# Two transformer blocks on one core: the feed-forward input takes its high weights over both halves of the activations in one product of 512 columns

## The chip, the cores and the metric

The kernel runs on one core of a Trainium2 chip. A time is the device time of one execution in microseconds (us), lower is better; three executions of the kernel before gave 1177.74, 1178.14 and 1179.59 us, so its median is 1178.14 us. The profile is of one further execution, with a time of its own.

## The reference, cut to what matters

Two transformer blocks follow each other on 256 tokens of width 1024. The first has a gated mixer, an attention and a lookup of expert rows; the second has three mixer branches and a feed-forward layer. Only that last layer is touched:

```python
n2 = rmsnorm(h, norm_ffn_pre[l])                                  # 256 x 1024
gu = n2 @ w_ffn_in[l]                                             # 1024 x 5632
ff = (jax.nn.silu(gu[..., :D_FF]) * gu[..., D_FF:]) @ w_ffn_out[l]  # D_FF = 2816
h = h + rmsnorm(ff, norm_ffn_post[l])
```

## The kernel before

**Split products.** Every weight and activation of the large products is float32 and is split in two: a high part, rounded to the type fp32r of TensorE (written by ScalarE, `w_hi`, `nT_hi`, `hT_hi`), and a low part, the rest (written by VectorE as a difference, `w_lo`, `nT_lo`, `hT_lo`). A product is three matmuls into one place of PSUM: high by high, high weights by low values, low weights by high values (`product`, L1818 to L1823).

**Weight blocks.** Weights come in blocks of 128 x 2048 numbers (1 MB). SP (the queue of SyncE) loads each into one of four slots of `wraw`, as soon as the block that stood there is split (`load_block`, L586). ScalarE rounds a block into one of three slots of `w_hi` (L772, "the cast") and VectorE writes `w_lo` beside it (L1228). The cast of a block must wait until TensorE has done with the block that used the slot three blocks earlier. TensorE starts a block when its `w_lo` is written (`w_split`).

**Feed-forward input.** There are 22 blocks `ff_in0` to `ff_in21`. Block j holds 128 channels of the gate half (a = 0) and 128 channels of the other half (a = 1, called "up" here), each with 8 chunks of 128 inputs. `channels_out` writes both into one PSUM bank, gate in columns 0 to 255 and up in columns 256 to 511; channels are on the partitions and the 256 tokens are the columns. Then ScalarE takes the silu of the gate (L1160), VectorE multiplies by the up half (`h32`, L1762, "the product" below), ScalarE rounds it (`hT_hi`, L1164, "the copy") and VectorE writes the rest (`hT_lo`, L1766).

**Order on ScalarE and VectorE.** Both execute strictly in the order in which the code issues. One turn j of the loop on ScalarE (L1155 to L1166) is: silu j, copy j - 1, cast of the block three places after `ff_in`j. One turn on VectorE (L1755 to L1769) is: product j, rest j - 1, `w_lo` of the block three places after. After turn 19 these blocks are `ff_out0`, `ff_out1` and so on.

**Feed-forward output.** 11 blocks `ff_out0` to `ff_out10`, each 24 matmuls of 512 columns (`rows_out`). Then the last norm and the store.

PSUM has eight banks; `psum_uses` hands them out in turn and `bank_full` / `bank_read` count for each bank how often it was filled and read. The kernel's functions around the change:

Of the kernel before, what the change touches and what calls it, by code (L numbers as in the profile page):

```python
# [13 lines left out]
P = 128  # L14
D = 1024
S = 256
# [62 lines left out]
def last_product(name):  # L79

    base, part = name[:-1], name[-1]
    if name in ("in2_x", "x_o"):
        return ("xq",) if name == "in2_x" else ("y_x", NT - 1, 1)
    if name.startswith(("in2_q", "in2_k")):
        return (name[4:5] + "2", int(part))
    if name.startswith("ff_in"):
        return ("ff", int(name[5:]))
    if name.startswith("ff_out"):
        return ("ff_out", NT - 1, 1) if name == f"ff_out{FC // 2 - 1}" else None
    if name.startswith(("pool_o", "sb_o")):  # L90
        return ("y_" + base[:-2], NT - 1, 1) if part == "1" else None
    if name in ("out1a", "out1b"):
        return ("w_out", 1, NT - 1) if part == "b" else None
    if part == "a":
        return None
    if name.startswith("in2_g"):
        return ("gate", int(name[5:-1]), NT - 1)
    if name in ("in2_vb", "in2_pb"):
        return (("v2", NT - 1) if name == "in2_vb" else ("pool_in", NT - 1))
    if name.startswith("out2_"):  # L100
        return ("w_out2", int(name[5:-1]), NT - 1)
    return ("proj" if name.startswith("in") else "w_out", int(name[-2]), NT - 1)
# [35 lines left out]
def psum_uses():  # L138

    uses, count, turn, held = {}, [0] * 8, {}, set()  # L140

    def use(*key, among=tuple(range(8))):
        free = [b for b in among if b not in held]
        n = turn.get(among, 0)
        while among[n % len(among)] not in free:
            n += 1
        b = among[n % len(among)]
        turn[among] = n + 1
        uses[key] = (b, count[b])
        count[b] += 1  # L150
        return b

    def both(name):
        for t in range(NT):
            for h in range(2):
                use(name, t, h)

    both("xT")
    for n in (1, 2, 3, 4):
        for t in range(NT):  # L160
            use("proj", n, t)
    for t in range(NT):
        for name in ("qT", "kT"):
            use(name, t)
    held.add(use("proj", 0, 0))
    use("score", 0)
    use("score", 1)
    held.add(use("proj", 0, 1))
    use("score", 2)
    use("pT", 0)  # L170
    use("pT", 1)
    held.remove(uses["proj", 0, 0][0])
    use("spatial", 0)
    for u in (3, 4):
        use("score", u)
    first = use("oT", 0)
    use("aT", 0)
    held.add(use("w_out", 0, 0))
    held.remove(uses["proj", 0, 1][0])
    use("pT", 2)  # L180
    use("score", 5)
    use("spatial", 1)
    held.add(use("w_out", 1, 0))
    for key in (("xbT", 0, 0), ("aT", 1), ("query0", 0), ("xbT", 0, 1), ("query0", 1)):
        use(*key)
    held.clear()
    use("pT", 3)
    use("route0")
    for key in (("w_out", 0, 1), ("w_out", 1, 1), ("oT", 1)):
        held.add(use(*key))  # L190
    for key in (("pT", 4), ("pT", 5), ("query1",), ("route1",)):
        use(*key)
    held.clear()
    for n in range(2):
        held.add(use("expert", 0, n))
    for h in range(2):
        use("xbT", 1, h)
    for j in [*range(EARLY, PEER_HEADS), *range(EARLY)]:
        use("query", j)
        use("route", j)  # L200
    first = set(held)
    for n in range(2):
        held.add(use("expert", 1, n))
    both("memT")
    use("mk")
    use("mv")
    held -= first
    both("nT")
    for t in range(NT):
        use("v2", t)  # L210
    held.clear()
    for key in ("q2", "k2"):
        for c in range(2):
            use(key, c)
    z_banks, sum_banks, one = (0, 1, 2, 3), (4, 5, 6), (7,)
    for i, name in enumerate(SLOT_BLOCKS):
        if pair_at(i, ATT_SLOT) is not None:
            use("sbT", pair_at(i, ATT_SLOT), among=one)
        if pair_at(i, Z_SLOT) is not None:
            for a in range(2):  # L220
                use("z", 2 * pair_at(i, Z_SLOT) + a, among=z_banks)
        if i in XS_SLOT:
            for j in range(2):
                use("xs", XS_SLOT.index(i), j, among=z_banks)
        if i in MIX_SLOT:
            use("mix", MIX_SLOT.index(i), among=one)
        if i in POOL_SLOT:
            use("poolT", POOL_SLOT.index(i), among=one)
        for h in heads_at(i, XO_SLOT)[::2]:
            use("xoT", h // 2, among=z_banks)  # L230
        for h in heads_at(i, XPT_SLOT):
            use("xpT", h, among=z_banks)
        if name == "in2_x":
            use("xq", among=sum_banks)
        elif name[-1] == "a":
            for t in range(NT):
                use(*slot_key(name, t), among=sum_banks)
    for key in ("y_x", "y_pool", "y_sb"):
        for t in range(NT):
            for n in range(2):  # L240
                use(key, t, n)
    both("mergedT")
    for t in range(NT):
        for n in range(2):
            use("w_out2", n, t)
    both("n2T")
    for j in range(FC):
        use("ff", j)
    for t in range(NT):
        for n in range(2):  # L250
            use("ff_out", t, n)
    return uses
# [26 lines left out]
def two_block_kernel(nc, io, out):  # L279
# [7 lines left out]
    with ExitStack() as ctx:  # L287
# [3 lines left out]
        def sem(name):  # L291
            return ctx.enter_context(nc.semaphore(name))
# [28 lines left out]
        def place(name, off, shape, dt=F32):  # L321
            size = 4
            for n in shape[1:]:
                size *= n
            assert off + size <= arena_bytes, name
            return nc.alloc_sbuf_tensor_at(name, shape, dt, offset=first_byte + off)
# [48 lines left out]
        w_apart = {"query2": (apart_prob[:, 1, :], apart_end[:, 2, :]), "query3": (apart_prob[:, 0, :], apart_prob[:, 2, :]),  # L375
                   "query6": (apart_keys[:, 0, :], apart_keys[:, 1, :]), "query7": (apart_end[:, 0, :], apart_end[:, 1, :])}

        nT_hi = place("nT_hi", 102 * KB, [P, KC, S], F32R)
        nT_lo = place("nT_lo", 110 * KB, [P, KC, S], F32R)
        gates = place("gates", 48 * KB, [P, NT, 3 * D])  # L380
        xqT = place("xqT", 70 * KB, [P, 2, S])
        sbT_hi = place("sbT_hi", 72 * KB, [P, 4, S], F32R)
# [20 lines left out]
        z_sb = place("z_sb", 92 * KB, [P, NT, D])  # L403
        silu = place("silu", 118 * KB, [P, 2, S])
        h32 = place("h32", 120 * KB, [P, 2, S])

        mkT = mkv[:, 0:2, :]
        mv = mkv[:, 2:4, :]
# [88 lines left out]
        h_ready = sem("h_ready")  # L497
        half_n2 = sem("half_n2")
        silu_ready = sem("silu_ready")
        product_rounded = sem("product_rounded")  # L500
        ffT_ready = sem("ffT_ready")

# [54 lines left out]
        def wait_full(eng, *key):  # L557

            b, u = at(*key)
            eng.wait_ge(bank_full[b], u + 1)  # L560
            return bank[b]
# [150 lines left out]
        def _(act):  # L712
# [441 lines left out]
            split_to("ff_in2")  # L1154
            for j in range(FC + 1):  # L1155
                if j < FC:
                    src = wait_full(act, "ff", j)
                    if j >= 2:
                        wait_read(act, "ff", j - 2)
                    nc.scalar.activation(silu[:, j % 2, :], src[:, 0:S], ACT.Silu).then_inc(silu_ready, 1)  # L1160
                if j >= 1:

                    wait_read(act, "ff", j - 1)
                    nc.scalar.copy(hT_hi[:, j - 1, :], h32[:, (j - 1) % 2, :]).then_inc(product_rounded, 1)  # L1164
                if j < FC:
                    split_ahead(f"ff_in{j}")  # L1166
# [12 lines left out]
        def _(dve):  # L1179
# [572 lines left out]
            for h in range(2):  # L1752
                rest_tile("n2T", nT_lo, nT_hi, 1, h)
            split_to("ff_in2")
            for j in range(FC + 1):  # L1755
                if j < FC:

                    dve.wait_ge(silu_ready, j + 1)
                    if j >= 2:
                        dve.wait_ge(ffT_ready, j - 1)  # L1760
                    src = bank[at("ff", j)[0]]
                    nc.vector.tensor_tensor(h32[:, j % 2, :], silu[:, j % 2, :], src[:, S:2 * S],  # L1762
                                            ALU.mult).then_inc(read_of("ff", j), 1)
                if j >= 1:
                    dve.wait_ge(product_rounded, j)
                    nc.vector.tensor_tensor(hT_lo[:, j - 1, :], h32[:, (j - 1) % 2, :], hT_hi[:, j - 1, :].bitcast(F32),  # L1766
                                            ALU.subtract).then_inc(ffT_ready, 1)
                if j < FC:
                    split_ahead(f"ff_in{j}")  # L1769
# [10 lines left out]
        def _(pe):  # L1780
# [503 lines left out]
                            turn_n2(0)  # L2284
            keep_warm(22, "n2T", 1, 0)
            turn_n2(1)
            for j in range(FC):
                channels_out(f"ff_in{j}", nT, "ff", j, turned="n2T" if j == 0 else None)
            for j in range(FC // 2):
                pe.wait_ge(ffT_ready, 2 * j + 2)  # L2290
                rows_out(f"ff_out{j}", (hT_hi, hT_lo), j == 0, j == FC // 2 - 1, 2 * j, lambda t, n: ("ff_out", t, n))
# [101 lines left out]
```

## Time and profile before

| quantity | value |
|---|---|
| median of three executions | 1178.14 us (1177.74 to 1179.59) |
| profiled execution, its own time | 1177.23 us |
| span of its trace | 1175.4 us |
| feed-forward input on TensorE, first matmul | 983.09 us from the start of the span |
| feed-forward output on TensorE, first and last matmul | 1109.89 and 1169.52 us |
| granted clock of TensorE, mean of the execution | 0.994 |

In what follows PE is TensorE, PEld its weight loads, DVE is VectorE, ACT is ScalarE, POOL is GpSimd. Times inside the execution count from the start of the span. Durations of matmuls in the profile are modelled and overlap each other; how fast TensorE works is read from the distance between starts. On DVE and ACT too, one instruction may start a little before the one ahead of it has ended in the records.

### The profile page before, as it was taken

The page shows a single profiled execution, that of the slowest core. Times are in us where ns is not written, and L with a number is a line of the kernel's source. Part 1 is how long each engine was busy: PE and PEld are TensorE (multiplying, and loading weights), DVE is VectorE, ACT ScalarE, POOL GpSimd, SP SyncE. Part 2 cuts the span into 40 slices and gives each one's busy share as a digit, 9 for nine tenths or more (in the row PEclk, how much of TensorE's full clock was granted, in tenths as well). Part 3 has the DMA queues.
Part 4 walks back from the last instruction along what each step waited for, and adds up shares of the span by engine and source line. Part 5 has one row for each costly group of instructions (what it writes and reads, how often), then busy time and mean ns, then how long its engine had stood idle before and what let it go on. Part 6 is the DMA issues. An engine that isn't in the chain of part 4 may idle for free.

```text
span 1175.4 us, 12637 instructions
## 1 busy us (share of the span) xinstructions
PE 1060.0 (90%) x4468; PEld 689.4 (59%) x4468; DVE 811.2 (69%) x1704; ACT 389.8 (33%) x724; POOL 272.4 (23%) x261
## 2 busy tenths in 40 slices
PE   8999699999998778798877777899999999999998
PEld 7888354544454233244322222359888878999986
DVE  5787868777877768787887776764555586555543
ACT  7674212202220111310211012045765445444532
POOL 0001345434444334433433433400000000000000
PEclk9999899999999999999999999999999999999999
DMA  9847999999999999999999999977434444555540
GB/s 346 337 168 270 393 375 398 422 421 421 422 420 422 421 421 421 421 421 421 418 420 422 410 421 416 421 271 267 144 143 144 162 161 161 180 180 181 183 174 36
DMA packets 55534, 371.91 MB, mean 316 GB/s; under 512 B 6192, under 2 KB 7344, under 8 KB 12080
## 3 DMA queue, kind: packets, MB, share of 16 engines
q0 software_dynamic: 36864, 268.45, 55.4%
q1 hardware_dynamic: 18608, 102.65, 23.7%
q8 instruction: 36, 0.59, 0.2%
q14 instruction: 26, 0.21, 0.0%
HBM read 370.03 MB, written 1.05 MB: 316 GB/s over the span
## 4 chain that ended last, share of the span: by engine, by line
PE 58%; DMA 29%; DVE 8%; issue 3%; ACT 1%; POOL 1%; DVEq 0%; POOLq 0%; ACTq 0%
DMA uv<-in_peer_uv,eidx 29%; PE bank L2123 13%; PE bank L1821 12%; PE bank L1823 12%; PE bank L1822 12%; PE bank L1893 4%; DVE uv L1509 3%; PE bank L1792 1%; DVE diag L1523 1%; POOL uv L696 1%; PE bank L2011 1%; DVE xn L1691 0%; DVE tmp L1684 0%; PE bank L1965 0%; PE bank L1932 0%
## 5 line engine op out<-in xcount | busy, mean ns | idle before, releaser
L2123 PE MATMUL bank<-uv,diag 128*128 128x512 f32 x1024 | 491.2, 608 | 100.4 <-DVE diag L1523 93.9
L1509 DVE SCALAR_TENSOR_TENSOR uv<-uv,xn 128x1024 f32<-128x1024 f32 x256 | 313.5, 1225 | 132.4 <-DMA uv<-in_peer_uv,eidx 129.9
L2123 PEld LDWEIGHTS bank<-uv,diag 128*128 128x128 f32 x1024 | 180.4, 191 | 375.9 <-issue 373.5
L696 POOL DMA_INDIRECT uv<-in_peer_uv,eidx x256 | 272.1, 1063 | 485.6 <-PE bank L2123 357.6
L1228 DVE TENSOR_TENSOR w_lo<-wraw,w_hi 128x2048 fp32r<-128x2048 f32 x71 | 162.3, 2290 | 119.5 <-ACT w_hi L772 119.4
L984 ACT ACTIVATE chosen<-chosen 128x1 f32<-128x1 f32 x256 | 51.8, 203 | 505.0 <-DVE uv L1509 504.7
L772 ACT CAST w_hi<-wraw 128x2048 fp32r<-128x2048 f32 x71 | 135.3, 1908 | 65.6 <-PE bank L1823 65.4
L1821 PE MATMUL bank<-nT_hi,w_hi 128*128 128x256 f32 x432 | 122.5, 284 | 0.8 <-DVE nT_lo L1249 0.8
L1822 PE MATMUL bank<-nT_lo,w_hi 128*128 128x256 f32 x432 | 122.3, 283 | 0.0
L1823 PE MATMUL bank<-nT_hi,w_lo 128*128 128x256 f32 x432 | 122.3, 283 | 0.0
L1523 DVE TENSOR_SCALAR diag<-const,chosen 128x128 f32<-128x128 f32 x256 | 89.1, 348 | 10.9 <-ACT chosen L984 10.7
L1821 PEld LDWEIGHTS bank<-nT_hi,w_hi 128*128 128x128 f32 x432 | 81.7, 189 | 1.2 <-issue 1.0
L1822 PEld LDWEIGHTS bank<-nT_lo,w_hi 128*128 128x128 f32 x432 | 81.7, 189 | 0.0
L1823 PEld LDWEIGHTS bank<-nT_hi,w_lo 128*128 128x128 f32 x432 | 81.7, 189 | 0.0
L1821 PE MATMUL bank<-w_hi,nT_hi 128*128 128x512 f32 x144 | 57.5, 399 | 0.3 <-DVE w_lo L1228 0.3
L1822 PE MATMUL bank<-w_lo,nT_hi 128*128 128x512 f32 x144 | 56.2, 390 | 0.0
L1823 PE MATMUL bank<-w_hi,nT_lo 128*128 128x512 f32 x144 | 56.1, 390 | 0.0
L1821 PE MATMUL bank<-w_hi,aT_hi 128*128 128x512 f32 x104 | 41.7, 401 | 2.3 <-DVE w_lo L1236 2.3
L1823 PE MATMUL bank<-w_hi,aT_lo 128*128 128x512 f32 x104 | 40.9, 393 | 0.0
L1822 PE MATMUL bank<-w_lo,aT_hi 128*128 128x512 f32 x104 | 40.8, 392 | 0.0
L1893 PEld LDWEIGHTS bank<-bT,wraw 128*128 128x128 f32 x192 | 30.3, 191 | 11.6 <-issue 9.7
L1893 PE MATMUL bank<-bT,wraw 128*128 128x128 f32 (+1 forms) x192 | 34.9, 327 | 0.0
(271 smaller groups left out, 1190.6 us busy)
## 6 DMA issues: line engine op xcount, KB each, us to landing
wraw<-in_ff_in SPq DMA_DIRECT2D x22, 1024.0 KB, 4.8
wraw<-in_ff_out SPq DMA_DIRECT2D x11, 1024.0 KB, 4.7
wraw<-in_query SPq DMA_DIRECT2D x4, 1024.0 KB, 5.2
uv<-in_peer_uv,eidx POOLq DMA_INDIRECT x256, 13.2
wraw<-in_in_q SPq DMA_DIRECT2D x2, 1024.0 KB, 9.0
wraw<-in_in_k SPq DMA_DIRECT2D x2, 1024.0 KB, 9.6
wraw<-in_pool_o SPq DMA_DIRECT2D x2, 1024.0 KB, 4.8
wraw<-in_sb_o SPq DMA_DIRECT2D x2, 1024.0 KB, 4.7
```

The lines of the kernel that those rows point to most:

```text
L696: pool.indirect_dma_start(out=uv[:, RING_AT[n % RING], :], out_offset=None, in_=io["peer_uv"], in_offset=bass.IndirectOffsetOnAxis(ap=eidx ...
L772: nc.scalar.copy(hi, raw).then_inc(w_rounded, 1)
L984: nc.scalar.activation(hgelu[head % 2][:, k:k + 1], hdot[head % 2][:, k:k + 1], ACT.Gelu_apprx_tanh).then_inc(hgelu_ready, 1)
L1228: nc.vector.tensor_tensor(lo, raw, hi.bitcast(F32), ALU.subtract).then_inc(w_split, 1)
L1509: nc.vector.scalar_tensor_tensor(out=u, in0=u, scalar=1.0, in1=xn[:, head // PEER_HEADS, :], op0=ALU.mult, op1=ALU.mult, accum_out=hdot[he ...
L1523: nc.vector.tensor_scalar(diag[:, n % RING, :], ident, hgelu[head % 2][:, k:k + 1], gate[head % 2][:, k:k + 1], ALU.mult, ALU.mult).then_i ...
L1792: mm = nc.tensor.transpose(dst[:, c * P:(c + 1) * P], src[:, c * P:(c + 1) * P], ident)
L1821: nc.tensor.matmul(dst, a_hi, b_hi, start=start, stop=False)
L1822: nc.tensor.matmul(dst, a_hi, b_lo, start=False, stop=False)
L1823: return nc.tensor.matmul(dst, a_lo, b_hi, start=False, stop=stop)
L1893: mm = nc.tensor.matmul(dst[:, a * width:(a + 1) * width], w[:, c * S + a * P:c * S + (a + 1) * P], aT[:, i % 2 * (KC // 2) + c, first:fir ...
L2123: mm = nc.tensor.matmul(acc[m][:, :], diag[:, n % RING, :], uv[:, RING_AT[n % RING], D + m * HALF:D + (m + 1) * HALF], start=(n % (ROWS // ...
```

## The change

High and low values now lie in one tile `nT_both` (same bytes as before; `nT_hi` and `nT_lo` are views of it). For a chunk, the high weights are used once, against high and low values together: one matmul of 2 x 256 = 512 columns. Its left 256 columns are high by high and its right 256 columns high weights by low values. The low weights make a second matmul of 256 columns that adds into the left half. The gate and the up half now take a bank each (44 uses of banks in place of 22). The two halves of a bank have to be summed: VectorE does that with one reduction per bank into `gate32` and `up32` in SBUF. The silu now reads `gate32`, the product reads `silu` and `up32`, and comes one turn later on VectorE than before.

```diff
@@ psum_uses
     for j in range(FC):
-        use("ff", j)
+        for a in range(2):
+            use("ff", j, a)
@@ ScalarE
             for j in range(FC + 1):
                 if j < FC:
-                    src = wait_full(act, "ff", j)
+                    wait_read(act, "ff", j, 0)
                     if j >= 2:
-                        wait_read(act, "ff", j - 2)
-                    nc.scalar.activation(silu[:, j % 2, :], src[:, 0:S], ACT.Silu).then_inc(silu_ready, 1)
+                        act.wait_ge(product_ready, j - 1)
+                    nc.scalar.activation(silu[:, j % 2, :], gate32[:, j % 2, :], ACT.Silu).then_inc(silu_ready, 1)
                 if j >= 1:
 
-                    wait_read(act, "ff", j - 1)
+                    act.wait_ge(product_ready, j)
                     nc.scalar.copy(hT_hi[:, j - 1, :], h32[:, (j - 1) % 2, :]).then_inc(product_rounded, 1)
@@ VectorE
-            for j in range(FC + 1):
+            for j in range(FC + 2):
                 if j < FC:
-
-                    dve.wait_ge(silu_ready, j + 1)
-                    if j >= 2:
-                        dve.wait_ge(ffT_ready, j - 1)
-                    src = bank[at("ff", j)[0]]
-                    nc.vector.tensor_tensor(h32[:, j % 2, :], silu[:, j % 2, :], src[:, S:2 * S],
-                                            ALU.mult).then_inc(read_of("ff", j), 1)
-                if j >= 1:
-                    dve.wait_ge(product_rounded, j)
-                    nc.vector.tensor_tensor(hT_lo[:, j - 1, :], h32[:, (j - 1) % 2, :], hT_hi[:, j - 1, :].bitcast(F32),
+                    for a, dst in ((0, gate32), (1, up32)):
+                        src = wait_full(dve, "ff", j, a)
+                        if not a and j >= 2:
+                            dve.wait_ge(silu_ready, j - 1)
+                            dve.wait_ge(product_ready, j - 1)
+                        nc.vector.tensor_reduce(dst[:, j % 2, :], src[:, :].rearrange("p (b k) -> p k b", b=2),
+                                                AX_X, ALU.add).then_inc(read_of("ff", j, a), 1)
+                if 1 <= j <= FC:
+                    dve.wait_ge(silu_ready, j)
+                    if j > 2:
+                        dve.wait_ge(ffT_ready, j - 2)
+                    wait_read(dve, "ff", j - 1, 1)
+                    nc.vector.tensor_tensor(h32[:, (j - 1) % 2, :], silu[:, (j - 1) % 2, :], up32[:, (j - 1) % 2, :],
+                                            ALU.mult).then_inc(product_ready, 1)
+                if j >= 2:
+                    dve.wait_ge(product_rounded, j - 1)
+                    nc.vector.tensor_tensor(hT_lo[:, j - 2, :], h32[:, j % 2, :], hT_hi[:, j - 2, :].bitcast(F32),
                                             ALU.subtract).then_inc(ffT_ready, 1)
                 if j < FC:
                     split_ahead(f"ff_in{j}")
@@ TensorE
+            def channels_wide(name, *key, turned=None):
+
+                w_hi, w_lo = split_block(name)
+                for a in range(2):
+                    dst = open_bank(*key, a)
+                    for c in range(KC):
+                        if turned and a == 0 and c % (KC // 2) == 0:
+                            half_ready(turned, c // (KC // 2))
+                        w = slice(c * S + a * P, c * S + (a + 1) * P)
+                        low = (dst[:, 0:S], w_lo[:, w], nT_hi[:, c, :])
+                        if c:
+                            nc.tensor.matmul(*low, start=False, stop=False, skip_group_check=True)
+                        mm = nc.tensor.matmul(two(dst[:, :]), w_hi[:, w], nT_both[:, :, c, :], start=(c == 0),
+                                              stop=(c == KC - 1), skip_group_check=True)
+                        if not c:
+                            nc.tensor.matmul(*low, start=False, stop=False, skip_group_check=True)
+                    mm.then_inc(full_of(*key, a), 1)
+
             for j in range(FC):
-                channels_out(f"ff_in{j}", nT, "ff", j, turned="n2T" if j == 0 else None)
+                channels_wide(f"ff_in{j}", "ff", j, turned="n2T" if j == 0 else None)
```

The order of instructions on VectorE (DVE), one turn of the feed-forward input in the kernel before; `w_lo` is the split of a coming weight block, `h` is `h32`:

```order
L1228 TENSOR_TENSOR w_lo<-wraw,w_hi 128x2048 [waits w_rounded]
L1762 TENSOR_TENSOR h_114<-silu,bank 128x256 [waits ffT_ready,silu_ready]
L1766 TENSOR_TENSOR hT_lo<-h_114,hT_hi 128x256 [waits product_rounded]
L1228 TENSOR_TENSOR w_lo<-wraw,w_hi 128x2048 [waits w_rounded]
L1762 TENSOR_TENSOR h_114<-silu,bank 128x256 [waits ffT_ready,silu_ready]
```

The same place on VectorE in the changed kernel (its own line numbers):

```order
L1232 TENSOR_TENSOR w_lo<-wraw,w_hi 128x2048 [waits w_rounded]
L1766 TENSOR_REDUCE gate_114<-bank 128x256 [waits product_ready,silu_ready,bank_full1]
L1766 TENSOR_REDUCE up_115<-bank 128x256 [waits bank_full2]
L1773 TENSOR_TENSOR h_113<-silu,up_115 128x256 [waits bank_read0,ffT_ready,silu_ready]
L1777 TENSOR_TENSOR hT_lo<-h_113,hT_hi 128x256 [waits product_rounded]
L1232 TENSOR_TENSOR w_lo<-wraw,w_hi 128x2048 [waits w_rounded]
```

Two reductions now stand between the split of a weight block and the product, and the product is that of the turn before.

ScalarE (ACT), two turns in the kernel before; the copy waits for the bank of the turn before to be read, which the product of that turn does:

```order
L1160 ACTIVATE silu<-bank 128x256 [waits bank_read3,bank_full5]
L1164 CAST hT_hi<-h_114 128x256 [waits bank_read4]
L772 CAST w_hi<-wraw 128x2048 [waits bank_full5,w_loaded0]
L1160 ACTIVATE silu<-bank 128x256 [waits bank_read4,bank_full6]
L1164 CAST hT_hi<-h_114 128x256 [waits bank_read5]
L772 CAST w_hi<-wraw 128x2048 [waits bank_full6,w_loaded1]
```

The same place on ScalarE in the changed kernel:

```order
L1164 ACTIVATE silu<-gate_114 128x256 [waits product_ready,bank_read7]
L1168 CAST hT_hi<-h_113 128x256 [waits product_ready]
L776 CAST w_hi<-wraw 128x2048 [waits bank_full0,w_loaded0]
L1164 ACTIVATE silu<-gate_114 128x256 [waits product_ready,bank_read1]
L1168 CAST hT_hi<-h_113 128x256 [waits product_ready]
L776 CAST w_hi<-wraw 128x2048 [waits bank_full2,w_loaded1]
```

The order stays; what moved is the origin of the waits: the copy waits for a product that VectorE issues in this same turn, behind both reductions, and the cast stands behind the copy.

## Rows read from the trace of the kernel before

**Rows 1.** The page: span, chain that ended last, loads to landing

```profile
span 1175.4 us, 12637 instructions
...
PE 58%; DMA 29%; DVE 8%; issue 3%; ACT 1%; POOL 1%; DVEq 0%; POOLq 0%; ACTq 0%
...
wraw<-in_ff_in SPq DMA_DIRECT2D x22, 1024.0 KB, 4.8
```

**Rows 2.** Stretches: us, PE, PEld, DVE, ACT, POOL busy (count), clock

```profile
983.30:1110.00 126.70, 126.70 (x1057) 126.70 (x1057) 68.50 (x65) 55.10 (x64) 0.00 (x0) 1.00 0.52 187
...
230.00:780.00 550.00, 462.15 (x1162) 198.84 (x1161) 419.03 (x1098) 100.22 (x302) 218.25 (x209) 1.00 1.00 413
```

**Rows 3.** Waits from 880 us on: total, times, longest

```profile
DVE w_lo L1228 <- ACT w_hi L772: 84.9, 41, 4.6
ACT silu L1160 <- PE bank L1823: 71.7, 22, 3.6
```

**Rows 4.** Timeline of PE: start, us, instruction

```profile
983.09 0.36 PE L1821 MATMUL bank<-nT_hi,w_hi 128*128 128x256 f32 x1 [0.83 <-DVE nT_lo L1249]
...
1109.89 0.40 PE L1821 MATMUL bank<-w_hi,hT_hi 128*128 128x512 f32 x1
...
1169.52 0.39 PE L1823 MATMUL bank<-w_hi,hT_lo 128*128 128x512 f32 x1
```

**Rows 5.** Groups by form, 870 to 1175 us: count, busy, mean ns

```profile
L1821 PE MATMUL bank<-nT_hi,w_hi 128*128 128x256 f32 x352 | 99.8, 283 | 0.8 <-DVE nT_lo L1249 0.8
```

**Rows 6.** Timeline of ACT, first turn and last turns

```profile
989.12 0.38 ACT L1160 ACTIVATE silu<-bank 128x256 f32<-128x256 f32 x1 [2.62 <-PE bank L1823]
989.40 1.90 ACT L772 CAST w_hi<-wraw 128x2048 fp32r<-128x2048 f32 x1
...
1110.09 0.38 ACT L1160 ACTIVATE silu<-bank 128x256 f32<-128x256 f32 x1 [3.27 <-PE bank L1823]
1110.37 0.40 ACT L1164 CAST hT_hi<-h 128x256 fp32r<-128x256 f32 x1
1110.66 1.91 ACT L772 CAST w_hi<-wraw 128x2048 fp32r<-128x2048 f32 x1
1112.47 0.40 ACT L1164 CAST hT_hi<-h 128x256 fp32r<-128x256 f32 x1
1112.89 1.28 ACT L756 ACT_TABLE_LOAD   x1
1114.18 0.20 ACT L756 ACTIVATE small<-eps 128x1 f32<-128x1 f32 x1
```

**Rows 7.** Timeline of DVE, before the first turn and last turns

```profile
984.72 4.49 DVE L1228 TENSOR_TENSOR w_lo<-wraw,w_hi 128x2048 fp32r<-128x2048 f32 x2 [1.11 <-ACT w_hi L772]
...
1110.50 0.42 DVE L1762 TENSOR_TENSOR h<-silu,bank 128x256 f32<-128x256 f32 x1 [1.37 <-ACT silu L1160]
1110.84 0.42 DVE L1766 TENSOR_TENSOR hT_lo<-h,hT_hi 128x256 fp32r<-128x256 f32 x1
1112.60 2.29 DVE L1228 TENSOR_TENSOR w_lo<-wraw,w_hi 128x2048 fp32r<-128x2048 f32 x1 [1.34 <-ACT w_hi L772]
1114.81 0.42 DVE L1766 TENSOR_TENSOR hT_lo<-h,hT_hi 128x256 fp32r<-128x256 f32 x1
```

**Rows 8.** Chain that ended last, before the first turn: start, us

```profile
976.86 0.76 DVE x_sb L1732
977.64 0.73 ACT junk L730 x2
...
982.25 0.70 DVE nT_lo L1249
983.09 0.36 PE bank L1821
```

**Rows 9.** Reductions on DVE: one in the timeline, two groups

```profile
45.58 0.69 DVE L1298 TENSOR_REDUCE qk_stat<-sq 128x8 f32<-128x512 f32 x1 [1.28 <-ACT sq L850]
46.19 0.16 DVE L1309 RECIPROCAL stat<-stat 128x2 f32<-128x2 f32 x1
...
L1498 DVE TENSOR_REDUCE small<-onehot 128x32 f32<-128x512 f32 x15 | 10.2, 679 | 0.0
...
L1659 DVE TENSOR_REDUCE xstat<-bank 128x2 f32<-128x512 f32 x4 | 2.7, 682 | 0.0
```

More of the change, by code:

```diff
@@ L86, in last_product @@
     if name.startswith("ff_in"):
-        return ("ff", int(name[5:]))
+        return ("ff", int(name[5:]), 1)
     if name.startswith("ff_out"):
@@ L376, in two_block_kernel @@
                    "query6": (apart_keys[:, 0, :], apart_keys[:, 1, :]), "query7": (apart_end[:, 0, :], apart_end[:, 1, :])}
-        nT_hi = place("nT_hi", 102 * KB, [P, KC, S], F32R)
-        nT_lo = place("nT_lo", 110 * KB, [P, KC, S], F32R)
+        nT_both = place("nT_both", 102 * KB, [P, 2, KC, S], F32R)
+        nT_hi, nT_lo = (nT_both[:, n, :, :] for n in range(2))
         gates = place("gates", 48 * KB, [P, NT, 3 * D])
@@ L405, in two_block_kernel @@
         h32 = place("h32", 120 * KB, [P, 2, S])
+        gate32 = place("gate32", 122 * KB, [P, 2, S])
+        up32 = place("up32", 124 * KB, [P, 2, S])
         mkT = mkv[:, 0:2, :]
@@ L499, in two_block_kernel @@
         silu_ready = sem("silu_ready")
+        product_ready = sem("product_ready")
         product_rounded = sem("product_rounded")
```

## The prediction

> **What bounds the kernel now.** I read the page first: the span is 1175.4 us and the chain that ended last is mostly PE, with the DMA of the expert rows next [rows 1]. The change touches only the feed-forward input, so I went to that stretch. There PE is busy all of the time, 126.70 of 126.70 us, at full clock [rows 2]. The waits say the same from the other side: ScalarE waits for PE 22 times, once in each turn, and VectorE waits for ScalarE's cast [rows 3]. PE waits for nobody in this stretch. So before the change this stage is worth what PE's instructions are worth, and it turns on how long the others stay ahead once PE is faster and they have more to do.
>
> **What PE gains.** From the first matmul of the input (983.09) to the first of the output (1109.89) there are 1056 matmuls of 256 columns (three groups of 352, of which [rows 5] shows one): 126.80 / 1056 = 0.1201 us from start to start [rows 4]. The output has 264 of 512 columns, 263 distances in 59.63 us: 0.2267 us each [rows 4]. One of 512 columns is thus 0.0135 us cheaper than two of 256. A block had 48 of 256 columns, 48 x 0.1201 = 5.76 us. It now has 16 of 512 and 16 of 256: 16 x 0.3468 = 5.55 us. Were PE still the bound, 22 x 0.215 = 4.7 us would be gained: 1173.4 us. The streamed columns are as many as before; only instructions are saved. That is small, so any new wait weighs against it.
>
> **What DVE and ACT get.** DVE gets two reductions of 512 elements per turn. Reductions of 512 elements take 679 ns with 32 outputs (from SBUF) and 682 ns with 2 outputs (from PSUM) [rows 9], so the price goes by what is read, not by the number of groups. The next instruction starts 0.61 us after such a reduction [rows 9]. I take 0.61 us for each; the lower bound is the step of an operation on 256 elements, 0.34 us (1110.50 to 1110.84 [rows 7]), if only outputs counted; the upper bound is two cycles per element read, 0.61 + 0.53 = 1.14 us, since no row here reads PSUM in steps of 256 elements (0.53 us is what 512 more elements would add: 2.29 us for 2048 and 0.42 us for 256 [rows 7] make 1.04 ns each). By sum of busy time all this fits: DVE has 2.21 + 0.34 + 0.34 + 1.22 = 4.1 us in a turn of 5.55. But the order doesn't let them be busy in parallel.
>
> **The loop that closes.** Follow one turn in the changed kernel. ACT's cast of a block; DVE's `w_lo` of that block; the two reductions; the product; ACT's copy, which waits for this product; ACT's next cast, which stands behind the copy. Each waits for the one before, and the last is the first of the next turn. Before the change the copy needed only the product of a turn earlier, so this ring was not closed within one turn. Its steps, start to start:
> - cast to `w_lo`: 1110.66 to 1112.60 = 1.94 us [rows 6, 7]
> - `w_lo` to gate reduction: 1112.60 to 1114.81 = 2.21 us [rows 7]
> - gate reduction, up reduction: 2 x 0.61 = 1.22 us [rows 9]
> - product to copy: 0.42 us and a handoff of 0.03 us (silu to `h`: 0.38 us long, 0.41 us later; DVE to ACT: an instruction of 0.75 us, 0.78 us later) = 0.45 us [rows 6 to 8]
> - copy to next cast: 1110.37 to 1110.66 = 0.29 us [rows 6]
>
> The sum is 6.11 us per turn. PE needs 5.55 us. So the ring, not PE, sets the pace as soon as the lead of the splits is used up. The silu (0.38 us) hides: it starts after the gate reduction, beside the up reduction and the product. The rest `hT_lo` hides under the cast. The wraw loads hide: a load lands in 4.8 us [rows 1], and has several turns.
>
> **When the lead ends.** DVE is busy with the two splits before the first turn until 984.72 + 4.49 = 989.21, so the gate reduction 0 starts at 989.13 (0.08 us of overlap, as in the step above), the silu at 989.84, the cast of `ff_in3` 0.28 us later at 990.12 (it was 989.40 [rows 6]), its `w_lo` at 992.06. Reductions of turn 1: 994.27 and 994.88; block 1 is done by 989.12 - 0.21 + 5.55 = 994.46, so they needn't wait. Product 0 at 995.49, copy 995.94, cast of `ff_in4` 996.23, `w_lo` 998.17 to 1000.46. From there every split is 6.11 us later: that of turn n ends at 994.35 + 6.11 n. PE wants that block at 988.91 + 5.55 (n + 2). The two meet at n = 10, so from `ff_in14` on PE waits about 0.56 us before each block. Turn 21 ends the split of `ff_out2` at 1122.66. Product 21 starts at 1122.58, copy 21 at 1123.03; then come the table load and its small activation, 1.93 us from the copy (1112.47 to 1114.18 and 0.22 [rows 6]), the cast of `ff_out3` at 1124.96, its `w_lo` from 1126.90 to 1129.19, and PE starts it 0.14 us later (a handoff from DVE to PE [rows 8]), at 1129.33. After it the ring is gone: a cast and a `w_lo` are 4.2 us against 5.44 us of PE per output block. Before, `ff_out3` started at 1109.89 + 3 x 5.44 = 1126.21. The difference is 3.1 us, and the tail behind it is unchanged.
>
> **Sum.** 1177.23 + 3.1 = 1180.3 us for the profiled execution; the median lies 0.9 us over it, so **1181.3 us**, 0.26% slower. All of PE's gain is spent waiting. Each 0.1 us in the ring is 20 to 21 times that at the end, 2.1 us: the result stands or falls with the step of a reduction.
>
> **A rule against the change.** [Rows 9] hold reductions over neighbours only. The Trainium skill, "Advanced Engine Details and Errata", section Memory Cachelines, says that PSUM is read in lines of 8 bytes and that accesses that aren't contiguous slow matmuls significantly. It speaks of matmuls, not of VectorE, and no row here shows such a read; taken over to VectorE in its hardest form it would put the reductions at my upper bound and the sum at the 1204 us of the second rival.
>
> **Rivals.**
> 1. Faster, 1173.4 us. The mechanism: a reduction with 256 outputs costs as an operation on 256 elements, step 0.34 us. Then the ring is 6.11 - 0.54 = 5.57 us, practically PE's 5.55; the splits never become late within 21 turns and the 4.7 us are kept. Against it: 682 ns for two outputs [rows 9]. The change breaks even at a ring of 5.96 us, a reduction step of 0.535 us. The chance is 0.1, other ways of loosening the ring included.
> 2. Much slower. The elements to be added lie 256 elements apart and DVE pays for each: up to 1.14 us, a ring of 7.17 us. That is 1.06 x 21 + 0.5 for the first turn, 22.8 us on top of 3.1: 1204 us. A part of that is as possible, from 1187 us on. The chance is 0.13.
> 3. About the same, 1176 to 1180.5 us: the ring closes at 5.85 to 6.07 us, for instance by a shorter handoff or overlap. The chance is 0.22, as 6.11 lies so close.
> 4. PE's clock falls with its pauses to 1.2 GHz, and a block takes some 11 us: over 1250 us. Against it: in the expert stage PE was busy 462 of 550 us and kept a clock of 1.00 [rows 2]; the new pauses are 9%. The chance is 0.02.
>
> **How the numbers follow.** The forecast, a ring of 6.07 to 6.35 us (the step of a reduction between 0.59 and 0.73 us, the latter if it had to be written before the next starts), gives 1180.5 to 1186.5 us and has 0.53. A measurement of this kernel tells about 0.2%, 2.4 us. Slower: forecast, rivals 2 and 4 = 0.68. Same: 0.22. Faster: 0.10. The range 1176 to 1190 us leaves out rival 1 (0.10), rival 4 and the larger part of rival 2 (0.09 together); it takes the lower part of rival 2 in.
>
> **What would show it.** In the trace after: `w_lo` of successive turns 6.1 us apart from turn 2 on; PE without idle time until about `ff_in13`, then a wait for DVE `w_lo` of 0.5 to 0.7 us at each block, 11 of them from `ff_in14` to `ff_out2`, and one of 1.1 us at `ff_out3`; ACT's copy waiting for DVE's product and no longer ACT's silu for PE; the reductions at 0.68 us each; 0.347 us for a pair of matmuls. Wrong would be: splits 5.55 us apart, with PE never waiting (rival 1), or reductions over 0.8 us (rival 2). If the pair of matmuls costs up to 6.1 / 16 = 0.38 us, the time doesn't change, since the ring covers it.

## The result, and the profile after

| | median, us | runs |
|---|---|---|
| before | 1178.17 (1176.32 to 1180.37) | 13 |
| after | 1181.42 (1180.33 to 1183.96) | 13 |

The ratio is 1.0028, 95% interval 1.0020 to 1.0037: the changed kernel is slower by 3.3 us, which is clear of noise. The prediction was 1181.3 us.

The page of the changed kernel: its span and the chain that ended last, beside [rows 1]:

```profile
span 1182.2 us, 11999 instructions
...
PE 47%; DMA 29%; DVE 11%; issue 8%; ACT 5%; POOL 1%; DVEq 0%; ACTq 0%; POOLq 0%
```

There are 638 instructions fewer, but PE's share of the chain fell from 58% to 47% and DVE's and ACT's grew from 9% to 16% together. "issue" grew because the chain books the time of DVE's split under it: in each turn of the stage it has 1.9 us for ACT's cast and then some 2 us of "issue" (1057.10 to 1059.08, for one) while DVE writes `w_lo`. So the two engines' real share of the chain is larger than 16%. The waits of PE's weight loads, of ACT and of DVE in the stage:

```profile
ACT silu L1164 <- DVE gate L1766: 65.5, 22, 3.4
DVE w_lo L1232 <- ACT w_hi L776: 62.5, 29, 3.5
...
ACT hT_hi L1168 <- DVE h L1773: 14.2, 22, 2.7
...
PEld bank L2310 <- DVE w_lo L1232: 3.7, 7, 0.6
```

Before [rows 3], ACT's silu waited for PE; now it waits for DVE, and so does the copy (`hT_hi`), 0.5 us in each turn. PE waits for the splits in seven input blocks, where it waited for nobody. One turn on DVE of the changed kernel (columns as in [rows 7]):

```profile
1050.78 2.29 DVE L1232 TENSOR_TENSOR w_lo<-wraw,w_hi 128x2048 fp32r<-128x2048 f32 x1 [1.94 <-ACT w_hi L776]
1052.99 0.68 DVE L1766 TENSOR_REDUCE gate<-bank 128x256 f32<-128x512 f32 x1
1053.59 0.68 DVE L1766 TENSOR_REDUCE up<-bank 128x256 f32<-128x512 f32 x1
1054.18 0.41 DVE L1773 TENSOR_TENSOR h<-silu,up 128x256 f32<-128x256 f32 x1
1054.52 0.42 DVE L1777 TENSOR_TENSOR hT_lo<-h,hT_hi 128x256 fp32r<-128x256 f32 x1
1056.88 2.29 DVE L1232 TENSOR_TENSOR w_lo<-wraw,w_hi 128x2048 fp32r<-128x2048 f32 x1 [1.94 <-ACT w_hi L776]
```

and the part of ACT that goes with the split at 1056.88:

```profile
1054.63 0.41 ACT L1168 CAST hT_hi<-h 128x256 fp32r<-128x256 f32 x1 [0.51 <-DVE h L1773]
1054.94 1.90 ACT L776 CAST w_hi<-wraw 128x2048 fp32r<-128x2048 f32 x1
```

Read the starts in turn: 1050.78 the split, 1052.99 and 1053.59 the reductions, 1054.18 the product, 1054.63 the copy, 1054.94 the cast, 1056.88 the next split. 6.10 us, with no slack anywhere between them; DVE sits idle for 1.94 us of it while ACT casts. That is the ring of the prediction.

In this first profile PE's clock fell at the start of the stage; in a second one of the same kernel (`after_again` below) it did not. The weight loads at the head of a block in it (the bracket is the wait before):

```profile
1060.43 0.19 PEld L2310 LDWEIGHTS bank<-nT_both,w_hi 128*128 128x128 f32 x1 [0.25 <-DVE w_lo L1232]
1066.54 0.19 PEld L2310 LDWEIGHTS bank<-nT_both,w_hi 128*128 128x128 f32 x1 [0.56 <-DVE w_lo L1232]
1072.64 0.19 PEld L2310 LDWEIGHTS bank<-nT_both,w_hi 128*128 128x128 f32 x1 [0.55 <-DVE w_lo L1232]
...
1103.15 0.19 PEld L2310 LDWEIGHTS bank<-nT_both,w_hi 128*128 128x128 f32 x1 [0.57 <-DVE w_lo L1232]
1109.28 0.19 PEld L1832 LDWEIGHTS bank<-w_hi,hT_hi 128*128 128x128 f32 x1 [0.57 <-issue]
...
1127.93 0.19 PEld L1832 LDWEIGHTS bank<-w_hi,hT_hi 128*128 128x128 f32 x1 [1.08 <-issue]
```

Eight input blocks wait, from 1060.43 to 1103.15, 6.10 us apart: these are `ff_in14` to `ff_in21`. Then `ff_out0` to `ff_out2` wait, and `ff_out3` waits 1.08 us. Ahead of `ff_in14` there is no such wait. In the four `ff_out` blocks the profile names no releaser ("issue"), but the split of each ended about 0.1 us before its weight load (that of `ff_out3` at 1127.82, for the load at 1127.93).

For the experiments I use, beside the medians, the length of the stage on PE: from the first matmul of the input to the last of the output. It leaves out the stages ahead, whose end moves by some microseconds between executions (the stage began at 981.96 us in one profile of the changed kernel and at 985.66 us in the other).

| profile | first input | last output | stage, us | clock in the first 4 us or so |
|---|---|---|---|---|
| before [rows 4] | 983.09 | 1169.52 | 186.43 | full |
| before_again | 983.00 | 1170.93 | 187.93 | fell |
| before_cast_first | 984.60 | 1172.51 | 187.91 | fell |
| after | 985.66 | 1176.24 | 190.58 | fell |
| after_again | 981.96 | 1171.34 | 189.38 | full |
| old_matmuls | 985.42 | 1174.83 | 189.41 | full |
| product_first | 983.98 | 1167.34 | 183.36 | full |
| no_reductions | 984.42 | 1167.18 | 182.76 | full |
| cast_first | 984.62 | 1168.90 | 184.28 | fell |
| cast_first_again | 983.18 | 1165.90 | 182.72 | full |
| third_reduction | 986.60 | 1189.15 | 202.55 | full |
| neighbours | 981.99 | 1171.41 | 189.42 | full |

With full clock on both sides the change costs 189.38 - 186.43 = 2.95 us; the sum had said 3.1. With the clock fallen on both sides it costs 190.58 - 187.93 = 2.65 us.

### The profile page after: what moved, and what is told of

Same layout as the page of the kernel before. It is cut to its first block, busy times and chain, and to the rows that moved or that the text cites. A ratio compares the mean times of both kernels' runs of the same rounds, so it can differ in the third digit from the quotient of the medians.

```text
span 1182.2 us, 11999 instructions
## 1 busy us (share of the span) xinstructions
PE 1061.2 (90%) x4116; PEld 670.9 (57%) x4116; DVE 835.4 (71%) x1748; ACT 392.7 (33%) x724; POOL 269.7 (23%) x261
## 4 chain that ended last, share of the span: by engine, by line
PE 47%; DMA 29%; DVE 11%; issue 8%; ACT 5%; POOL 1%; DVEq 0%; ACTq 0%; POOLq 0%
DMA uv<-in_peer_uv,eidx 29%; PE bank L2134 13%; PE bank L1832 8%; PE bank L1833 7%; PE bank L1834 7%; PE bank L1904 4%; ACT w_hi L776 4%; DVE uv L1513 3%; DVE gate L1766 1%; PE bank L1803 1%; DVE up L1766 1%; DVE diag L1527 1%; PE bank L2310 1%; DVE w_lo L1232 1%; DVE h L1773 1%
## 5 line engine op out<-in xcount | busy, mean ns | idle before, releaser
L700 POOL DMA_INDIRECT uv<-in_peer_uv,eidx x256 | 269.3, 1052 | 491.4 <-PE bank L2134 364.4
L2310 PE MATMUL bank<-nT_both,w_hi 128*128 128x512 f32 x352 | 123.4, 401 | 2.3 <-DVE w_lo L1232 1.4
L2309 PE MATMUL bank<-nT_both,w_lo 128*128 128x256 f32 x308 | 86.6, 281 | 0.0
L2310 PEld LDWEIGHTS bank<-nT_both,w_hi 128*128 128x128 f32 x352 | 64.2, 190 | 16.9 <-DVE w_lo L1232 3.7
L2309 PEld LDWEIGHTS bank<-nT_both,w_lo 128*128 128x128 f32 x308 | 58.9, 191 | 2.0
L1832 PE MATMUL bank<-w_hi,nT_both 128*128 128x512 f32 x144 | 57.5, 399 | 0.3 <-DVE w_lo L1232 0.3
L1834 PE MATMUL bank<-w_hi,nT_both 128*128 128x512 f32 x144 | 56.2, 390 | 0.0
L1833 PE MATMUL bank<-w_lo,nT_both 128*128 128x512 f32 x144 | 56.2, 390 | 0.0
L1832 PE MATMUL bank<-w_hi,hT_hi 128*128 128x512 f32 x88 | 34.6, 393 | 1.8 <-DVE w_lo L1232 1.5
L1834 PE MATMUL bank<-w_hi,hT_lo 128*128 128x512 f32 x88 | 34.3, 390 | 0.0
```

What stands on the lines that cost most here:

```text
L700: pool.indirect_dma_start(out=uv[:, RING_AT[n % RING], :], out_offset=None, in_=io["peer_uv"], in_offset=bass.IndirectOffsetOnAxis(ap=eidx ...
L1832: nc.tensor.matmul(dst, a_hi, b_hi, start=start, stop=False)
L1833: nc.tensor.matmul(dst, a_hi, b_lo, start=False, stop=False)
L1834: return nc.tensor.matmul(dst, a_lo, b_hi, start=False, stop=stop)
L2309: nc.tensor.matmul(*low, start=False, stop=False, skip_group_check=True)
L2310: mm = nc.tensor.matmul(two(dst[:, :]), w_hi[:, w], nT_both[:, :, c, :], start=(c == 0), stop=(c == KC - 1), skip_group_check=True)
```

## The experiments

### cast_first: open the ring on ScalarE

```diff
                     nc.scalar.activation(silu[:, j % 2, :], gate32[:, j % 2, :], ACT.Silu).then_inc(silu_ready, 1)
+                if j < FC:
+                    split_ahead(f"ff_in{j}")
                 if j >= 1:
                     act.wait_ge(product_ready, j)
                     nc.scalar.copy(hT_hi[:, j - 1, :], h32[:, (j - 1) % 2, :]).then_inc(product_rounded, 1)
-                if j < FC:
-                    split_ahead(f"ff_in{j}")
```

> Only ScalarE's order within a turn changes: silu j, cast of the coming block, then copy j - 1 (before: silu, copy, cast). Ring theory: the cast no longer waits for the product, and what is left from one w_lo to the next is 2.21 (w_lo) + 0.71 (gate reduction to silu) + 0.32 (silu to cast) + 1.94 (cast to w_lo) = 5.18 us, less than the 5.55 us of TensorE. TensorE is the bound again and the time is that of the kernel before less 22 x 0.215 us: 1173.5 us. Rival, the amount of added VectorE work and PSUM reads is what costs, not its place: no change, 1181.4 us. Rival, TensorE gains nothing by its new products: 1178.2 us.

Measured: 1174.52 us (6 runs) against 1178.44 us of the kernel before (21 runs), ratio 0.9966 (0.9953 to 0.9979). Every instruction of the changed kernel is still there; two of ScalarE's stand in another order. So neither the amount of VectorE's work nor its reads of PSUM set the time of the changed kernel, but the order in which ScalarE waited for them. On DVE in `cast_first`:

```profile
1038.76 2.29 DVE L1232 TENSOR_TENSOR w_lo<-wraw,w_hi 128x2048 fp32r<-128x2048 f32 x1 [0.64 <-ACT w_hi L776]
1040.97 0.68 DVE L1766 TENSOR_REDUCE gate<-bank 128x256 f32<-128x512 f32 x1
1042.36 0.69 DVE L1766 TENSOR_REDUCE up<-bank 128x256 f32<-128x512 f32 x1 [0.71 <-PE bank L2310]
...
1044.36 2.29 DVE L1232 TENSOR_TENSOR w_lo<-wraw,w_hi 128x2048 fp32r<-128x2048 f32 x1 [0.64 <-ACT w_hi L776]
```

A turn is 5.60 us and the up reduction waits for PE: PE is the bound again. A second profile, to have one without the fall of the clock:

> cast_first once more for a second profile: from the first matmul of the input to the last of the output 184.3 us if the clock falls in the first block as in its first profile, about 183.0 us if it doesn't; turns of 5.60 us in both cases.

Its stage is 182.72 us, and PE and its weight loads wait for nobody in it. Its first splits also show the opened ring by itself, before PE's pace holds it back: they start at 987.02, 992.19, 997.36 and 1002.53 us, 5.17 us apart where 5.18 was worked out; from 1007.80 on they are 5.59 or 5.60 us apart. It took 1173.61 us (one run).

### product_first: shorten the ring on VectorE

```diff
-                if j < FC:
-                    for a, dst in ((0, gate32), (1, up32)):
...
                 if 1 <= j <= FC:
                     dve.wait_ge(silu_ready, j)
...
                                             ALU.mult).then_inc(product_ready, 1)
+                if j < FC:
+                    for a, dst in ((0, gate32), (1, up32)):
...
```

> Only VectorE's order within a turn changes: product j - 1 stands ahead of the two reductions of turn j. The same work. Ring theory: the ring now runs over the gate reduction and the silu, 2.21 + 0.34 + 0.71 + 0.32 + 0.31 + 1.94 = 5.83 us a turn in place of 6.11. The lead of the splits lasts almost to the end (0.28 x 21 = 5.9 us of 5.7), and the last wait, at ff_out3, is some 1.7 us: 1175.5 us. Rival, the amount of work on VectorE costs: 1181.4 us.

Measured: 1175.94 us (11 runs), ratio 0.9979 (0.9970 to 0.9988). Two splits in a row on DVE:

```profile
1039.51 2.29 DVE L1232 TENSOR_TENSOR w_lo<-wraw,w_hi 128x2048 fp32r<-128x2048 f32 x1 [1.65 <-ACT w_hi L776]
...
1045.32 2.29 DVE L1232 TENSOR_TENSOR w_lo<-wraw,w_hi 128x2048 fp32r<-128x2048 f32 x1 [1.66 <-ACT w_hi L776]
```

5.81 us where the longer ring had 6.10 and 5.83 was worked out. The lead lasted: the only wait of PE that the profile has is at `ff_out3` (0.7 us before its weight load). The stage is 0.6 us longer than that of `cast_first_again`.

### old_matmuls: the changed kernel with the old work on TensorE

```diff
-                        mm = nc.tensor.matmul(two(dst[:, :]), w_hi[:, w], nT_both[:, :, c, :], start=(c == 0),
+                        nc.tensor.matmul(dst[:, 0:S], w_hi[:, w], nT_hi[:, c, :], start=(c == 0),
+                                         stop=(c == KC - 1), skip_group_check=True)
+                        mm = nc.tensor.matmul(dst[:, S:2 * S], w_hi[:, w], nT_lo[:, c, :], start=False,
                                               stop=(c == KC - 1), skip_group_check=True)
```

> The changed kernel with each product of 512 columns cut into its two of 256 columns (same banks, same reductions, same waits): 48 matmuls of 256 columns a block, 5.76 us as before the change. Ring theory: TensorE waits less but the splits come at the same times, 6.11 us apart, so the time stays that of the changed kernel: 1181.3 us, within 0.5 us. Rival, TensorE is still the bound somewhere in the stage and the new wait adds to it: 1181.4 + 4.7 = 1186.1 us, or a part of that.

Measured: 1181.72 us (10 runs), ratio 1.0026 (1.0016 to 1.0037). The stage is 189.41 us, that of `after_again` 189.38. TensorE has 16 matmuls more in each of 22 blocks and nothing moves. In the changed kernel, then, the gain of the new products is wholly spent waiting, and the result is that of the reductions and their waits alone.

### no_reductions: TensorE's part alone

```diff
@@ ScalarE
-                    wait_read(act, "ff", j, 0)
+                    src = wait_full(act, "ff", j, 0)
...
-                    nc.scalar.activation(silu[:, j % 2, :], gate32[:, j % 2, :], ACT.Silu).then_inc(silu_ready, 1)
+                    nc.scalar.activation(silu[:, j % 2, :], src[:, 0:S], ACT.Silu).then_inc(read_of("ff", j, 0), 1)
...
@@ VectorE, in the order of the kernel before
...
+                    nc.vector.tensor_tensor(h32[:, j % 2, :], silu[:, j % 2, :], src[:, 0:S],
+                                            ALU.mult).then_inc(read_of("ff", j, 1), 1)
```

> TensorE's part of the change alone: the new products and two banks per block, but no reductions; silu reads the left half of the gate bank, the product the left half of the up bank, in the order of the kernel before. It leaves out the addition of high weights times low values. Both theories on the ring agree that TensorE bounds: 5.55 us a block, 1173.5 us. If the new products save less than 0.0135 us per pair in a stream, it is nearer 1178.2 us; that tells the size of the first term by itself.

Measured: 1173.82 us (5 runs), ratio 0.9959 (0.9947 to 0.9972). From the first input matmul (984.42) to the first output matmul (1107.55) are 123.13 us, 5.60 us a block, or 0.350 us for a pair of matmuls where 0.347 was worked out. The input took 126.80 us before, so the gain is 126.80 - 123.13 = 3.7 us and not 4.7. `cast_first_again`, with all its reductions, has the same stage, 182.72 against 182.76 us: there the reductions are hidden entirely.

### third_reduction: more of the suspected cost

```diff
                 if j < FC:
+                    src = wait_full(dve, "ff", j, 0)
+                    ...
+                    nc.vector.tensor_reduce(spare32[:, j % 2, :], src[:, :].rearrange("p (b k) -> p k b", b=2),
+                                            AX_X, ALU.add)
                     for a, dst in ((0, gate32), (1, up32)):
```

> The changed kernel with one reduction more in each turn of VectorE (the gate bank once more, into a spare tile), ahead of the two. Ring theory: each turn is 0.60 us longer, 6.70 us, and of the lead of the splits nothing else changes: 21 x 0.60 = 12.6 us over the changed kernel, 1194.0 us. Rival, the loss has another cause (the start of the stage, the clock, the tail): the VectorE has 1.4 us of idle time in each turn of the changed kernel and the added reduction goes there, 1181.4 us.

Measured: 1194.62 us (4 runs) against 1178.09 us of the kernel before (13 runs), ratio 1.0140 (1.0117 to 1.0163). Splits on DVE:

```profile
1043.09 2.29 DVE L1233 TENSOR_TENSOR w_lo<-wraw,w_hi 128x2048 fp32r<-128x2048 f32 x1 [1.95 <-ACT w_hi L777]
1045.30 0.68 DVE L1765 TENSOR_REDUCE spare<-bank 128x256 f32<-128x512 f32 x1
...
1049.79 2.29 DVE L1233 TENSOR_TENSOR w_lo<-wraw,w_hi 128x2048 fp32r<-128x2048 f32 x1 [1.95 <-ACT w_hi L777]
```

6.70 us a turn. The 1.95 us in which DVE waits for the cast (the expectation put this idle time at 1.4 us) stay as long as they were: the reduction doesn't go into them but pushes them back. 202.55 - 189.38 = 13.2 us is 22 times 0.60, one turn more than was expected.

### neighbours: the distance between the elements that are added

```diff
-                        nc.vector.tensor_reduce(dst[:, j % 2, :], src[:, :].rearrange("p (b k) -> p k b", b=2),
+                        nc.vector.tensor_reduce(dst[:, j % 2, :], src[:, :].rearrange("p (k b) -> p k b", b=2),
```

> The changed kernel with the reductions adding neighbours (elements 2k and 2k + 1 of the bank) in place of elements k and 256 + k. It computes other sums, with the same reads, writes and counts. If the distance of 256 elements costs VectorE anything, the reductions of the changed kernel (683 ns) are longer than these, and the time falls by 21 times twice the difference. I expect 682 ns here too and the time of the changed kernel, 1181.4 us.

Its reductions, and then those of `after_again` (count, busy, mean ns):

```profile
L1766 DVE TENSOR_REDUCE gate<-bank 128x256 f32<-128x512 f32 x22 | 15.0, 683 | 0.0
L1766 DVE TENSOR_REDUCE up<-bank 128x256 f32<-128x512 f32 x22 | 15.0, 680 | 0.0
```

```profile
L1766 DVE TENSOR_REDUCE gate<-bank 128x256 f32<-128x512 f32 x22 | 15.0, 683 | 0.0
L1766 DVE TENSOR_REDUCE up<-bank 128x256 f32<-128x512 f32 x22 | 15.0, 680 | 0.0
```

The same to the nanosecond. Its median is 1180.35 us (10 runs), ratio 1.0024 (1.0012 to 1.0036), which the interval doesn't tell from the changed kernel's 1.0028, and its stage is 189.42 us against 189.38.

### before_cast_first: the order alone

The two ScalarE statements of `cast_first` exchanged in the kernel before:

```diff
                     nc.scalar.activation(silu[:, j % 2, :], src[:, 0:S], ACT.Silu).then_inc(silu_ready, 1)
+                if j < FC:
+                    split_ahead(f"ff_in{j}")
                 if j >= 1:
                     wait_read(act, "ff", j - 1)
                     nc.scalar.copy(hT_hi[:, j - 1, :], h32[:, (j - 1) % 2, :]).then_inc(product_rounded, 1)
-                if j < FC:
-                    split_ahead(f"ff_in{j}")
```

> The kernel before with ScalarE's order of cast_first (silu j, cast of the coming block, copy j - 1) and nothing else. Ring theory: there TensorE never waits in this stage, so the order is worth nothing by itself: 1178.2 us, within 1 us. Rival, the order is a gain of its own, and cast_first owes its time to it and not to the new products: 1174.5 us.

Measured: 1177.16 us (12 runs) against 1178.06, ratio 0.9991 (0.9982 to 1.0000). That is within what this measurement can tell from nothing, and far from 1174.5. Its stage is 187.91 us with the clock fallen, that of `before_again`, fallen too, 187.93. The order pays only together with the new products.

### after_again and before_again: the clock in the first block

> The changed kernel once more, for a second profile. In its first profile TensorE's granted clock was 0.58 from 986 to 990 us, in the first block of the input, and the block ended some 1.3 us later than I had worked out. If this belongs to the change it is seen again; if it comes and goes it may be absent. The turns of VectorE are 6.10 us in both cases.

> The kernel before once more, for a second profile, to see whether the clock falls in its first block of the input too. In the profile at hand it did not. Blocks are 5.76 us in both cases.

They took 1179.04 and 1178.64 us, one run each. The stretches of the changed kernel in its first profile (columns as in [rows 2]; the clock stands after POOL's count):

```profile
985.66:989.66 4.00, 4.00 (x14) 3.48 (x15) 2.89 (x3) 3.39 (x2) 0.00 (x0) 0.57 0.00 0
...
990.00:1114.10 124.10, 122.38 (x690) 104.70 (x688) 84.14 (x99) 52.33 (x59) 0.00 (x0) 1.00 0.51 182
```

its second profile, where the clock did not fall:

```profile
981.96:985.96 4.00, 4.00 (x23) 3.52 (x24) 2.88 (x3) 3.40 (x2) 0.00 (x0) 1.00 0.00 0
```

and the kernel before in its second:

```profile
983.00:987.00 4.00, 4.00 (x21) 4.00 (x22) 2.89 (x3) 3.40 (x2) 0.00 (x0) 0.57 0.00 0
987.00:1111.30 124.30, 124.30 (x1039) 124.30 (x1038) 65.81 (x63) 51.86 (x62) 0.00 (x0) 1.00 0.54 191
```

Four microseconds of the changed kernel hold 14 matmuls in its first profile and 23 in its second. The fall comes and goes, in both kernels. It isn't part of the change.

## Why the prediction was right

**What bounds.** PE alone before the change: `no_reductions` takes 3.7 us of work from PE, and the stage is 3.7 us shorter. After the change it is the ring, shown by `old_matmuls` (more work on PE, no change), by `third_reduction` (each 0.60 us in the ring is paid in full) and by `cast_first` (the same work, ring open, 3.9 us less than the kernel before).

**The ring.** 6.11 us were forecast and 6.10 measured. Its steps are 1.94, 2.21, 0.60 + 0.59, 0.45 and 0.31 us, each within 0.02 us of what was read from the trace of before. The disputed term, the reduction, was priced by rows of reductions with 2 and 32 outputs; with 256 outputs it is 683 and 680 ns. Rival 1, a price by outputs, falls by this. Rival 2, a price for the distance, falls by `neighbours`. The Trainium skill, "Advanced Engine Details and Errata", section Memory Cachelines, has accesses in PSUM that aren't contiguous slow down matmuls. Taken over to VectorE's reductions, of which that section does not speak, it doesn't hold here, by the equal groups above; no run here tests it for matmuls.

**The lead.** `ff_in14` was to be the first block that waits, and is, in the profile with full clock; with it 8 input blocks wait, then `ff_out0` to `ff_out2`, and `ff_out3` waits 1.08 us (1.1 forecast).

**PE's gain: mis-sized.** The step "a block now has 16 of 512 and 16 of 256: 16 x 0.3468 = 5.55 us" took both distances from streams of one kind. In the new stream a pair takes 0.350 us, a block 5.60, and the gain is 3.7 us, not 4.7. The excess sits in the matmuls of 512 columns: in `no_reductions`, from 1000 to 1050 us, the next matmul starts on average 232 to 234 ns after one of 512 (0.2267 us was taken) and 115 or 116 ns after one of 256 (0.1201 us was taken). The error had no weight in the forecast, since the ring covers it, but rival 1 would have given 1174.4 us and not 1173.4, and `cast_first` was expected 1.0 us too fast for this reason. Why a matmul of 512 columns is longer here stays open. It isn't the alternation alone, as the step is 232 ns also where one of 512 follows another. The new product reads its columns in two pieces, `nT_hi` and `nT_lo`, where the output's reads one; no run separates this.

**The sum.** 3.1 us were forecast for the stage; 2.95 us came with full clock in both, and the medians differ by 3.25 us. Most of the 0.15 us between lies in the last turn: from the split of `ff_out2` to that of `ff_out3` 6.53 us were worked out and 6.41 measured. The closeness of the median owes something to luck: executions of one kernel spread by 3 to 4 us, and the forecast's own range reached from 1180.5 to 1186.5 us. Two small slips change nothing: the instruction of the handoff is 0.76 us long in [rows 8], not 0.75, and 1181.3 us is 0.27% over 1178.14, not 0.26%.

**Rival 4.** PE's pauses of 0.56 us in each turn didn't lower its clock: 1.00 from 990 to 1114 us. Rival 3, a ring a little shorter, was 0.03 us away: at 6.07 us in place of 6.10 the time would have been within the 0.2% that the prediction called the same.

## What to carry to other kernels

Work that fits an engine's idle time by sum can still set the pace. When work is added to an engine, follow the orders of all engines through one turn of the loop and see whether a chain now leads back to its own start within the turn; its length is the sum of start-to-start distances in the trace, and it is compared with the bound's turn, not with busy shares. Where such a ring closes, moving one statement can open it: here the cast ahead of the copy turned 0.28% slower into 0.34% faster (1174.52 us, the lowest median here of a kernel that leaves nothing of the computation out). A lead of some blocks delays the cost but doesn't pay it: the first 14 input blocks ran here without a wait of PE. By this account a stage with few turns would have shown little of the loss; no run here has such a stage.

## What the runs showed of the hardware

- TensorE's clock fell to its lower level (1.2 GHz; 0.57 as the mean of the first 4 us) at the start of the stage in four of twelve profiles: the changed kernel, `before_again`, `cast_first` and `before_cast_first`. Ahead of it TensorE had run 22 filler products (44 instructions in the trace) in 5.1 us, paused 0.8 us, transposed a tile and paused 0.8 us again, in these as in the other eight. The stage is 1.5 us longer for it in the kernel before (187.93 against 186.43), 1.2 us in the changed one, 1.6 us in `cast_first`. What decides it stays open.
- A reduction of 512 float32 elements takes 678 to 686 ns on VectorE with 2 to 256 outputs; one of 256 elements with 16 outputs takes 420 ns (`before`).
- A silu of 256 columns takes 384 ns from PSUM before the change and 418 ns from SBUF after it. It was hidden.
